# Reordering VectorE's low parts and splitting the heads' square sums in two fp32r parts on GpSimd

## The reference

```python
# feed-forward, both layers
u = rmsnorm(x) @ w_up
x = x + (silu(conv(gate)) * up) @ w_down
# gated linear attention, layer 1, for each head's output o (256 channels)
o = o * rsqrt(mean(o * o) + EPS) * norm_w
o = o * silu(g)
x = x + o @ w_o
```

## Time and profile before

| | |
|---|---|
| median of 3 runs | 1090.58 us (1089.57 to 1090.9) |
| the profiled execution | 1091.51 us |
| its span, first to last instruction | 1089.7 us |
| TensorE busy | 1070.5 us, 98% of the span |
| VectorE, ScalarE, GpSimd busy | 752.5, 492.9, 116.4 us |
| granted TensorE clock | 0.996 of full speed |
| instructions | 15616 |

### The profile page before, as it was taken

One profiled execution on the slowest core, in us unless ns is written; L12 is line 12 of the kernel. 1 busy time (PEld: TensorE's weight loads), 2 busy tenths in 40 slices (PEclk: granted clock), 3 DMA queues, 4 the chain that ended last, 5 costly groups with the idle time before them and its releaser, 6 DMA issues.

```text
span 1089.7 us, 15616 instructions
## 1 busy us (share of the span) xinstructions
PE 1070.5 (98%) x5892; PEld 917.6 (84%) x5892; DVE 752.5 (69%) x1095; ACT 492.9 (45%) x763; POOL 116.4 (11%) x109
## 2 busy tenths in 40 slices
PE   7999999999999999999999999999999999999996
PEld 5888788888899888898888888888888899888896
DVE  5588667767875667787644556867676876667786
ACT  6366554434433334454652345454444533334452
POOL 3100040000100000123021221030000100000122
PEclk9999999999999999999999999999999999999998
DMA  6512042226643225552222211132226652225542
GB/s 196 162 59 78 2 135 97 97 96 183 156 135 106 97 97 168 139 147 80 95 78 96 79 39 58 62 112 97 97 96 183 159 162 96 97 96 168 132 122 90
DMA packets 43371, 121.10 MB, mean 111 GB/s; under 512 B 5202, under 2 KB 10098, under 8 KB 43316
## 3 DMA queue, kind: packets, MB, share of 16 engines
q1 hardware_dynamic: 34736, 106.45, 29.5%
q0 software_dynamic: 4608, 11.54, 6.5%
q10 hardware_dynamic: 3972, 2.38, 1.2%
HBM read 116.93 MB, written 2.88 MB: 110 GB/s over the span
## 4 chain that ended last, share of the span: by engine, by line
PE 93%; DVE 4%; DMA 1%; ACT 1%; issue 0%; SPq 0%; DVEq 0%
PE PS L464 68%; PE PS L522 18%; PE PS L637 1%; PE PS L655 1%; DMA DRAW_W<-w_down 1%; PE PS L645 1%; DMA X<-xT 1%; PE PS L787 1%; DVE X L1863 1%; PE PS L819 0%; PE PS L806 0%; PE PS L790 0%; PE PS L821 0%; PE PS L716 0%; PE PS L743 0%
## 5 line engine op out<-in xcount | busy, mean ns | idle before, releaser
L464 PE MATMUL PS<-XH,WH 128*128 128x512 f32 x992 | 393.2, 396 | 7.4 <-DVE XL L1333 7.3
L464 PE MATMUL PS<-XH,WL 128*128 128x512 f32 x992 | 387.6, 391 | 0.0
L464 PE MATMUL PS<-XL,WH 128*128 128x512 f32 x992 | 387.3, 390 | 0.0
L464 PEld LDWEIGHTS PS<-XH,WH 128*128 128x128 f32 x992 | 187.0, 189 | 49.5 <-issue 10.6
L464 PEld LDWEIGHTS PS<-XH,WL 128*128 128x128 f32 x992 | 187.0, 189 | 39.4
L464 PEld LDWEIGHTS PS<-XL,WH 128*128 128x128 f32 x992 | 187.2, 189 | 38.9 <-issue 1.0
L910 ACT CAST WH<-WRAW 128x1024 fp32r<-128x1024 f32 x137 | 142.6, 1044 | 165.4 <-DMA WRAW<-w_up 109.8
L1316 DVE TENSOR_TENSOR WL<-WRAW,WH 128x1024 fp32r<-128x1024 f32 x137 | 172.9, 1262 | 22.2 <-ACT WH L910 21.6
L1354 DVE TENSOR_TENSOR GS<-PS,R 128x512 f32<-128x512 f32 x44 | 30.4, 692 | 116.8 <-PE PS L464 116.8
L522 PE MATMUL PS<-AH,DH_Z 128*128 128x256 f32 x352 | 98.1, 279 | 1.0 <-DVE X L1449 0.8
L522 PE MATMUL PS<-AH,DL_Z 128*128 128x256 f32 x352 | 97.4, 277 | 0.0
(11 more groups left out here) (232 smaller groups left out, 1501.1 us busy)
## 6 DMA issues: line engine op xcount, KB each, us to landing
WRAW<-w_up SPq DMA_DIRECT2D x88, 512.0 KB, 3.3
WRAW<-w_bin SPq DMA_DIRECT2D x24, 512.0 KB, 3.2
DRAW_W<-w_down SPq DMA_DIRECT2D x24, 384.0 KB, 3.9
DRAW_W<-w_down SPq DMA_DIRECT2D x24, 320.0 KB, 3.3
WRAW<-w_qkv SPq DMA_DIRECT2D x11, 512.0 KB, 4.5
WSUM_Z<-w_down SPq DMA_DIRECT2D x12, 384.0 KB, 4.7
WSUM_Z<-w_down POOLq DMA_DIRECT2D x12, 384.0 KB, 6.3
WSUM_Z<-w_down SPq DMA_DIRECT2D x12, 320.0 KB, 3.9
```

Source lines behind the costliest of these rows:

```text
L464: last = mm(PS[:, bank], w[:, c:c + P], x[:, kb], start=start and n == 0 and w is wh and x is hi, stop=stop and n == len(kbs) - 1 and w is wl)
```

## The change

Four edits:

- In `down_rounds`, for the round in which X becomes final (n = 7), Z1's take goes ahead of X's low part 0 and Z2's take ahead of low part 1; low part 2 follows W22's. X's low parts 3 to 7 and the low parts of the units B_V and B_V+1 move to `ffn`: low parts 3 and 4 before W12's take, B_V's behind it, 5 to 7 behind W22's take, then B_V+1's. Where no X becomes final the order stays.
- In the last head's turn the third output unit's low part goes ahead of `head_norm(2)`, and the fourth output unit's ahead of `head_lo(2)`.
- `head_sum` on GpSimd has two more instructions of 128x512: a copy of the sum to SSH in fp32r, and the difference to SSL, also fp32r. The copy waits until the ones product before has read SSH and SSL.
- `head_square` on TensorE waits for the second of them and does two fp32r matmuls, with SSH and SSL, in place of one fp32 matmul.

```diff
--- before.py
+++ after.py
@@ -278,6 +278,7 @@
         a_done, am_ready, kut_done, kut_ready = sem("a_done"), sem("am_ready"), sem("kut_done"), sem("kut_ready")
         u_done, st_ready, o_done, o_ready = sem("u_done"), sem("st_ready"), sem("o_done"), sem("o_ready")
         hsum_ready, hms_done, hstd_ready = sem("hsum_ready"), sem("hms_done"), sem("hstd_ready")
+        hsum_hi, hsum_lo = sem("hsum_hi"), sem("hsum_lo")
         sg_ready, y_ready, yh_ready, yl_ready = sem("sg_ready"), sem("y_ready"), sem("yh_ready"), sem("yl_ready")
         t_ready, nt2_ready, gated_ready = sem("t_ready"), sem("nt2_ready"), sem("gated_ready")
         t1_ready, ah_last, al_last = sem("t1_ready"), sem("ah_last"), sem("al_last")
@@ -823,10 +824,11 @@
                     last.then_inc(o_done, 1)
 
             def head_square(h):
-                pe.wait_ge(hsum_ready, h + 1)
+                pe.wait_ge(hsum_lo, h + 1)
                 if h < 3:
                     pe.wait_ge(am_ready, h + 2)
-                mm(PS[:, B4], ONES, SQ[:, 0], start=True, stop=True).then_inc(hms_done, 1)
+                mm(PS[:, B4], ONESR[:], SSH[:], start=True, stop=False)
+                mm(PS[:, B4], ONESR[:], SSL[:], start=False, stop=True).then_inc(hms_done, 1)
 
             for h in range(BH):
                 head_scores(h)
@@ -1571,25 +1573,20 @@
                 take_w22(m - 1)
                 weight_lo(m, "W12")
                 weight_lo(m, "Z3")
+                take_z1(m)
                 if st is not None:
                     x_lo(st, 0)
-                take_z1(m)
+                take_z2(m)
                 if st is not None:
                     x_lo(st, 1)
-                    x_lo(st, 2)
-                take_z2(m)
                 weight_lo(m, "W22")
                 if st is not None:
-                    x_lo(st, 3)
+                    x_lo(st, 2)
                 take_z4(m)
-                if next_unit is not None:
+                if next_unit is not None and st is None:
                     lo_unit(next_unit)
-                if st is not None:
-                    x_lo(st, 4)
                 take_z3(m)
-                if st is not None:
-                    x_lo(st, 5)
-                if next_unit is not None:
+                if next_unit is not None and st is None:
                     lo_unit(next_unit + 1)
 
             def ffn(layer, st):
@@ -1611,10 +1608,14 @@
                 up_steps(layer, 1)
                 down_rounds(n + 4, None if layer else st + 1, None if layer else B_V)
                 if layer == 0:
+                    x_lo(st + 1, 3)
+                    x_lo(st + 1, 4)
                     take_w12(n + 7)
+                    lo_unit(B_V)
                     take_w22(n + 7)
-                    x_lo(st + 1, 6)
-                    x_lo(st + 1, 7)
+                    for m in range(5, KT_D):
+                        x_lo(st + 1, m)
+                    lo_unit(B_V + 1)
                     lo_unit(B_V + 2)
 
             first = slice(0, FIRST)
@@ -1824,11 +1825,14 @@
                 states(h)
                 dve.wait_ge(unit_done, u + 2)
                 tt(SG[:, 2 * h + 1], PS[:, 1], R[:], ALU.mult).then_inc(unit_evac, 1)
+                if h == BH - 1:
+                    lo_unit(u + 4)
                 if h >= 1:
                     head_norm(h - 1)
-                lo_unit(u + 4)
+                if h < BH - 1:
+                    lo_unit(u + 4)
+            lo_unit(B_O + 3)
             head_lo(2)
-            lo_unit(B_O + 3)
             head_norm(3)
             head_lo(3)
             lo_unit(B_O + 4)
@@ -1982,6 +1986,14 @@
                 pool.wait_ge(o_ready, 2 * h + 2)
                 nc.gpsimd.tensor_tensor(SQ[:, 0], SQ[:, 0], SQ[:, 1], ALU.add).then_inc(hsum_ready, 1)
                 pool.wait_ge(hsum_ready, h + 1)
+                if h == 0:
+                    pool.wait_ge(ms_done, 3)
+                else:
+                    pool.wait_ge(hms_done, h)
+                nc.gpsimd.tensor_copy(SSH[:], SQ[:, 0]).then_inc(hsum_hi, 1)
+                pool.wait_ge(hsum_hi, h + 1)
+                nc.gpsimd.tensor_tensor(SSL[:], SQ[:, 0], SSH[:].bitcast(F32), ALU.subtract).then_inc(hsum_lo, 1)
+                pool.wait_ge(hsum_lo, h + 1)
 
             for h in range(BH):
                 pool.wait_ge(a_done, h + 1)
```

## The result

The changed kernel took 1092.86 us (median of 12 runs, 1091.66 to 1094.7) against 1090.16 (1089.26 to 1091.88, 12 runs) for the kernel before: a ratio of 1.0023, interval 1.0015 to 1.003, which is 2.5 us more, 1.6 to 3.3. The forecast was 1092.0 and +1.4. The sign was right, and both intervals lie above 1, so the changed kernel is slower, by some 0.2%. The size is at the upper end of the forecast's own range.

What follows compares the result with a forecast made beforehand. TensorE, busy 1070.5 of 1089.7 us, bounds the kernel. The terms -1.3 - 0.41 + 1.23 + 1.23 + 0.6 = +1.35, say +1.4, give 1092.0 us; range 1089.2 to 1094.2, the forecast's own 1091.0 to 1093.2.

Steps and rivals of the forecast that it cites:

- X stage: Layer 0's last down round: Z4 starts right behind Z2, gaining 1.3 us, bounds 0 to 1.43.
- First square: First head's square sum: VectorE idle, so GpSimd finishes in time; no TensorE stall, 0.41 us gained.
- Second and third square: Those heads' square sums: GpSimd alternates with VectorE, TensorE idles 1.64 us, less 0.41: a loss of 1.23 each.
- Output stage: Third unit's wait goes, but the stretched last norm brings new waits: TensorE leaves about 0.6 us later.
- The bound of 1.1 gained: Output stage's best case: 1.1 us gained if GpSimd's new work did not meet the norm.
- (a): Rival: no exclusion for the new GpSimd pair, so -2.8 us, 1087.8, faster; chance 0.11.
- (b): Rival: VectorE goes first, or the reciprocal excludes too; +3.6 us, 1094.2; chance 0.18.
- (c): Rival: X's gain taken over by the sixth low part or mean square; +2.7 us, 1093.3; chance 0.11.
- (d): Rival: half the exclusion, 0.5 us lost per square, output stage even; -0.7 or so, 1089.9 to 1091; chance 0.14.

Runs made afterwards that it cites:

- e7: Changed kernel with TensorE keeping the fp32 square; GpSimd's copy and subtraction run unused. One execution, 1091.17 us.
- e9: Changed kernel with a plain fp32 square, without copy and subtraction, for the last head only. One execution, 1089.9 us.
- e2: Kernel before with VectorE's order of the last head's turn alone, fp32 squares kept: 1090.32 us, ratio 0.9993.
- e10: Kernel before with the X stage's and last head's orders and ScalarE's fourth output unit high part earlier, no two-part squares: 1089.13 us, ratio 0.9983.
- e8: Changed kernel with VectorE's low parts of an earlier head moved behind the gate unit's evacuation, square sum unmoved. One execution, 1093.12 us.
- e1: Kernel before with the X stage's reordering alone: 1089.98 us against 1090.87, ratio 0.9993.
- e6: Changed kernel with later squares, earlier head's low parts behind gate evacuation, last head's square plain fp32, ScalarE's fourth output unit high part earlier: 1087.92 us, ratio 0.9976.
- e11: Changed kernel with later squares, earlier head's low parts behind gate evacuation, ScalarE's fourth output unit high part earlier, all four pairs. One execution, 1089.88 us.
- e12: Changed kernel measured again: 1092.73 us against 1090.86, ratio 1.0018. Its theory 2: something else of 1 us belongs to the change, in a stretch outside the three stages.
- e4: Changed kernel with the square sum of heads 0 to 2 behind the first half of the next gate unit: 1090.76 us, ratio 1.0000.

## Why the prediction came out as it did

**X stage: right.** Forecast -1.3, shown -1.36, of which up to 0.4 is chance of the profiled execution before. VectorE's next late item was the sixth low part, as said, and cost 0.07.

**First square: right.** GpSimd ended its three instructions at 632.63 beside an idle VectorE, TensorE's square ran at 632.73 without a wait, and from the gate evacuation just before it to the next one VectorE needed 0.38 less (7.70 in place of 8.08). The forecast was 0.41.

**Second and third square: right, 0.06 and 0.09 low.** Forecast +1.23 each, out of a wait of 1.64. From evacuation to evacuation around them the changed kernel needs 1.29 and 1.32 more (20.69 and 20.72 in place of 19.40). The waits themselves are 1.43 and 1.42, and behind each the next matmul starts 0.11 later than in steady state (653.42 to 653.76 is 0.34, against 0.23). From the add's end to the subtraction's the forecast had 3.27; it took 3.22 (650.15 to 653.37). The order forecast for the collision holds row by row: low part, copy, YL, subtraction.

**Output stage: right, sum and steps.** Forecast +0.6, measured +0.51: VectorE idle 1.6 (1.64), TensorE 1.0 before the fourth unit (0.82) and 0.7 before the last quarter (0.26). Both of TensorE's waits are shorter than forecast. Counted from the first output product, TensorE wanted the last head's low part 0.25 later than I had it (18.20 in place of 17.95) and got it 0.1 earlier (18.46 in place of 18.55); as the part's arrival sets the end of the stage, only the 0.1 counts. e7 and e9 show that the pair beside the norm, and not the new order, is the cost. The bound of 1.1 gained is not tested: e2 and e10 gained 0.75 without the 0.41 of the fourth square, and no run has that 0.41 without GpSimd's load.

**Rivals.** (a), no exclusion, falls with the rows above and with e8, where taking VectorE's instruction away shortened the subtraction by 0.32. Of (b), VectorE never went twice while GpSimd waited, and the reciprocal does not exclude: GpSimd's add started at 686.04, during a reciprocal that lasted from 683.42 to 686.77, and ran for 1.29, its free length; had it been excluded it could not have ended before 687.9. The page GPSIMD Engine Reference of the Trainium skill (Key points) names VectorE instructions with two SBUF inputs, or in a 2-port mode, as those that contend. On the reciprocal, which no row of before could show, the trace agrees. (c) came true for 0.07 of its 1.3. (d), half the exclusion, falls too: the copy and the subtraction each met one of VectorE's instructions, at 1.3 us a head and not 0.5.

**What was missed.** The sum of the stages is -1.36 + 2.23 + 0.51 = +1.38, and the forecast's terms make +1.35. The measured +2.5 and +2.0 are larger. A step that the prediction does not have gives part of it: it took the time outside the span to be unchanged. It went from 1.8 to 2.1 (2.09 to 2.18 in twelve runs of the changed kernel; 1.73 to 1.84 in the 27 runs of the kernel before that stand beside e1), +0.3. With the chance 0.4 of before's X stage the sum is +2.1, within both intervals. What the 0.3 is was not found. It came with the fourth pair: e6 and e9 have three pairs and 1.8, e7 has four unused ones and 2.1, though the last pair ends some 400 us before the span does.

The profiles show a second part that the prediction does not have. TensorE's 256-column products start 0.113 us apart or 0.118 apart. In both profiles of the changed kernel the slower pace stands from 890 to 920, in layer 1's first down chunk, behind one product that starts 0.11 late, and costs 1.2 and 1.3 us; in the kernel before that stretch has the faster one. The chain of waits from 880 to 925, of the kernel before and of the changed one:

```profile
879.91 37.97 PE PS L522 x335
```
```profile
879.98 40.22 PE PS L523 x344
```

That is 0.1133 a product against 0.1169, the faster pace's first ten microseconds included. e11 has the slower pace there too, and no other run has. So theory 2 of e12 is half right: the stretch exists in both profiles of the changed kernel, but not in them alone. The kernel before has the slower pace elsewhere, from 1051 to 1074, where it costs 0.9, and every profile has it somewhere, in changing places, at 30 to 556 of 1843 steps from product to product. Each long stretch of it begins behind a product that starts at least 0.06 late; but many late starts are followed by the faster pace. What sets it was not found, and two profiles do not say whether the changed kernel has it at 890 in most executions. How much of the measured 2.0 to 2.5 is due to it stays open.

**The expectation of e4** failed at a step that the prediction too passed over: the pair was priced by what waits for its result, and what it delays on VectorE was priced in the output stage only. In the heads a second chain (YL, SG, ScalarE's KUT, state updates) stood behind the first. Removing the first wait showed it: TensorE then waited 0.51 for the second, twice, and heads came out 1.6 above the -1.15 that the squares alone would give.

## What to carry to other kernels

Before you give an idle engine a new instruction, look at what the engine that takes turns with it does at that time, and add both prices: what waits for the result, and what that other engine then delivers late. Here replacing 0.41 us of TensorE by 2 us of GpSimd paid only after two instructions of VectorE had moved out of the way and the reader had been put half a unit later. Where a wait is removed, ask for the second chain behind it: here it took back 1.6 of the 3.4 us that the removal should have gained.

## What the runs showed of the hardware

- On these tiles GpSimd and VectorE take turns when VectorE has two SBUF inputs. An add of 128x512 takes 1.29 free and 1.5 to 2.2 in turns, a one-input copy 0.61 free and 0.96 or 1.49, VectorE's low part of 128x512 0.68 free and 1.09, 1.42 (e6) or 1.75. That GpSimd's one-input copy has to wait as well had been assumed from its add and is shown here.
- The reciprocal and the evacuation from PSUM ran beside GpSimd at their own length (3.35 and 0.69), and GpSimd beside them at its own (add 1.29, subtraction 1.27).
- TensorE's 256-column products run on at one of two paces, 0.113 or 0.118 us, over tens of microseconds, at a granted clock of 1.00 in both (after, 900 to 920; before, 900 to 910). The cause was not found.
- Profiles differ by up to 1.4 us in stages that no edit touches. In e1's profile one raw weight of the down projection came late, and TensorE waited 1.15 at 321.38, where before it did not (e4's waits 1.03 at the same product, e6's 0.71, the other profiles' not at all):

```profile
312.10 4.75 DMA DRAW_W<-w_down
```
```profile
321.38 0.38 PE L522 MATMUL PS<-AH,DH_W 128*128 128x256 f32 x1 [1.15 <-DVE X L1449]
```

  So a difference of one profiled span says nothing at this size, and the stages have to be cut out.
